# One program for the output projection, the queries, the search and the expert rows of a two-layer hybrid block

## The reference, cut to what matters

```
x = x + mod[2] * (y @ w_out[l])
h2 = modulate(x, norm2_g[l], mod[3], mod[4])       # rms_norm * g * (1 + scale) + shift
q = (h2 @ wq).reshape(tb, 8, 2, 64)                # 8 heads, two halves
s1, s2 = q[:, :, 0] @ subkeys[0].T, q[:, :, 1] @ subkeys[1].T
v1, i1 = top_k(s1, 16);  v2, i2 = top_k(s2, 16)
top, pos = top_k(v1[:, None] + v2[None, :], 16)    # 16 of 256 candidates
eid = i1 * 128 + i2 at pos                         # 8 * 16 = 128 experts for a token
gate = softmax(top)
act = gelu(h2 . u[eid])
x = x + mod[5] * sum(gate * act * v[eid])
```

## Time and profile before

| | us |
|---|---|
| median of 3 runs (lowest, highest) | 5564.36 (5556.88, 5573.46) |
| the profiled execution, its time | 5550.64 |
| the profiled execution, its span | 5548.8 |
| DVE, PE, POOL busy in that span | 2761.7, 2600.2, 2996.4 |
| mean granted TensorE clock | 0.698 |

### The profile page before, as it was taken

How to read it: one execution, slowest core, us unless ns; L and a number is a source line. 1 busy time by engine, 2 the same in 40 slices (tenths; PEclk the granted TensorE clock), 3 DMA queues, 4 the chain that set the end, 5 groups by cost and what they waited for, 6 DMA issues and landing times. The chain is left out here.

```text
span 5548.8 us, 34331 instructions
## 1 busy us (share of the span) xinstructions
PE 2600.2 (47%) x10865; PEld 1112.8 (20%) x10865; DVE 2761.7 (50%) x6111; ACT 493.1 (9%) x1044; POOL 2996.4 (54%) x2702
## 2 busy tenths in 40 slices
PE   6976787203333333333333569668600333333344
PEld 2435554100000000000000134355400000000001
DVE  1136644896556466465443011554598655644410
ACT  0025430000000000000000000443000000000000
POOL 1001201687777777777777620130178777777765
PEclk9987998656565565666666789789855655565567
DMA  5401011799999999999999941011189999999998
GB/s 187 144 23 18 2 40 50 278 336 378 387 377 378 377 370 375 377 378 385 376 380 365 365 169 61 8 19 40 43 311 329 366 361 371 363 371 367 369 367 322
DMA packets 450113, 1468.11 MB, mean 265 GB/s; under 512 B 59226, under 2 KB 97326, under 8 KB 446862
## 3 DMA queue, kind: packets, MB, share of 16 engines
q0 software_dynamic: 368640, 1342.34, 64.1%
q1 hardware_dynamic: 70280, 99.62, 5.6%
q10 hardware_dynamic: 11014, 23.95, 1.4%
HBM read 1459.62 MB, written 6.13 MB: 264 GB/s over the span
## 5 line engine op out<-in xcount | busy, mean ns | idle before, releaser
L1738 DVE CUSTOM_DVE_ANT_0 peer_U<-peer_U,peer_H 128x1024 f32<-128x1024 f32 x1280 | 1564.4, 1223 | 1326.5 <-DMA peer_U<-in_peer_u_dram,peer_expert 1235.4
L1704 PE MATMUL tile_acc<-peer_V,peer_spread 128*32 128x512 f32 x4544 | 977.2, 998 | 1821.4 <-DMA peer_V<-in_peer_v_dram,peer_turned 1730.7
L1603 POOL DMA_INDIRECT peer_U<-in_peer_u_dram,peer_expert x1280 | 1376.9, 1076 | 571.5 <-issue 389.3
L1618 POOL DMA_INDIRECT peer_V<-in_peer_v_dram,peer_turned x1136 | 1253.5, 1103 | 490.3 <-issue 329.2
L1704 PEld LDWEIGHTS tile_acc<-peer_V,peer_spread 128*32 128x32 f32 x4544 | 190.0, 153 | 2538.0 <-issue 2537.4
L371 PE MATMUL proj_acc<-proj_w,HT 128*128 128x512 f32 (+2 forms) x1280 | 485.7, 539 | 2.9 <-DVE PR L426 2.9
L741 POOL MEMSET glascore_Q<- 128x8192 f32 x2 | 13.8, 6925 | 559.5 <-POOLq L101 559.5
L371 PEld LDWEIGHTS proj_acc<-proj_w,HT 128*128 128x128 f32 x1280 | 241.6, 190 | 244.2 <-issue 213.1
L1281 POOL TENSOR_TENSOR X<-X,out_part 128x512 f32<-128x512 f32 x20 | 25.3, 1265 | 457.4 <-DVE out_part L1271 457.4
L426 DVE COPY PR<-proj_acc 128x512 f32<-128x512 f32 (+2 forms) x80 | 49.5, 622 | 404.6 <-PE proj_acc L371 404.6
L1430 PE MATMUL tile_keys<-peer_sub,peer_QT 64*128 64x128 f32 x256 | 37.6, 442 | 406.4 <-DVE peer_rest L1448 330.0
(11 more groups left out here) (261 smaller groups left out, 3305.5 us busy)
## 6 DMA issues: line engine op xcount, KB each, us to landing
peer_ada<-in_ada_w_dram SPq DMA_DIRECT2D x24, 1024.0 KB
proj_w<-in_w_in_dram SPq DMA_DIRECT2D x10, 2048.0 KB, 8.0
peer_U<-in_peer_u_dram,peer_expert POOLq DMA_INDIRECT x1280
peer_V<-in_peer_v_dram,peer_turned POOLq DMA_INDIRECT x1136
proj_ada<-in_ada_w_dram ACTq DMA_DIRECT2D x16, 1024.0 KB, 4.8
setup_ada<-in_ada_w_dram SPq DMA_DIRECT2D x8, 1024.0 KB, 17.3
out_w<-in_w_out_dram SPq DMA_DIRECT2D x2, 4096.0 KB, 14.8
query_w<-in_peer_wq_dram SPq DMA_DIRECT2D x4, 2048.0 KB, 15.9
```

What stands on the lines that cost most here:

```text
L1603: pool.indirect_dma_start(s.U[:, n % RING], None, u_rows, bass.IndirectOffsetOnAxis(ap=s.expert[:, j % 2, k:k + 1], axis=0)).then_inc(ug[n ...
L1618: pool.indirect_dma_start(place, None, v_rows, bass.IndirectOffsetOnAxis(ap=s.turned[:, i % 2, e:e + 1], axis=0)).then_inc(done, 16)
L1704: mm = nc.tensor.matmul(acc[32 * c:32 * c + 32, i % 2, half], s.spread[:, e * 32:e * 32 + 32], v_slot(V * GROUP + c)[0][:, 512 * half:512 ...
L1738: nc.vector.tensor_tensor_reduce(out=s.U[:, n % RING], in0=s.U[:, n % RING], in1=s.H[:, tiles[j]], scale=1.0, scalar=0.0, op0=ALU.mult, op ...
```

## The change

`out_project`, `peer`, `peer_queries` and `peer_tiles` become one stage `experts`; `norm_modulate` stays for the input projection only. `layer` calls it while Y is allocated:

```diff
-        out_project(nc, m, l, t0, Y)
-        if stop == "out":
-            return
-    peer(nc, m, l, t0)
+        experts(nc, m, l, t0, Y)
```

The rings lend their memory to the weights (`w_out` lies in U, `wq` in V), H is written over Y, and PSUM banks are shared. The loads stand in one SP stream; POOL waits for the last output product and the first tile's expert numbers:

```diff
+        w_out, wq = s.U, s.V
+        s.H = Y
+        out_acc, turn = acc[:, 0], acc[:, 1]
+        order = [("y", 0), ("y", 1), ("h", 0), ("y", 2), ("h", 1), ("y", 3), ("h", 2)]
+        for i in range(4, T):
+            order += [("y", i), ("h", i - 1)]
+        order += [("h", T - 1)]
+        place = {what: n for n, what in enumerate(order)}
...
             def _(pool):
+                pool.wait_ge(prods, 2 * T)
                 for n in range(FIRST_V + V_ALL):
                     j, k = n // SLOTS, n % SLOTS
-                    if n == 2 * RING:
-                        nc.gpsimd.memset(s.spread[:], 0.0).then_inc(zeroed, 1)
+                    if n == ZERO_AT:
+                        pool.wait_ge(qprods, 2 * T)
+                        nc.gpsimd.memset(s.spread, 0.0).then_inc(zeroed, 1)
                     if n < U_ALL:
-                        if j and k == 0:
-                            pool.wait_ge(sems.chosen, j)
+                        if k == 0:
+                            pool.wait_ge(sems.chosen, j + 1)
...
             def _(sp):
+                sp.dma_start(gain[:], row_bcast(m.a["diff_norm_g"][l])).then_inc(gains, 16)
+                for half, sem in ((0, w_in), (1, w_in2)):
+                    cols = slice(512 * half, 512 * half + 512)
+                    sp.dma_start(w_out[:, :, cols], m.a["w_out"][l].rearrange("(k p) n -> p k n", p=P)[:, :, cols]).then_inc(sem, 16)
+                for x in range(2):
+                    sp.dma_start(gate_row[:, x], row_bcast(mod_row(m, l, 1 - x, 2))).then_inc(gate_in, 16)
+                sp.dma_start(sub_rows, m.a["peer_subkeys"][l].rearrange("s n d -> n s d")).then_inc(key_in, 16)
+                sp.dma_start(g, row_bcast(m.a["norm2_g"][l])).then_inc(coef_in, 16)
+                for x, stream in enumerate(norm_streams):
+                    sp.dma_start(sc[:, x], row_bcast(mod_row(m, l, 1 - stream, 4))).then_inc(coef_in, 16)
+                for x, stream in enumerate(norm_streams):
+                    sp.dma_start(sh[:, x], row_bcast(mod_row(m, l, 1 - stream, 3))).then_inc(shift_in, 16)
+                for half, sem in ((0, wq_in), (1, wq_in2)):
+                    cols = slice(512 * half, 512 * half + 512)
+                    sp.dma_start(wq[:, :, cols], m.a["peer_wq"][l].rearrange("(k p) n -> p k n", p=P)[:, :, cols]).then_inc(sem, 16)
```

PE has a list written out by hand. `project_out(i, half)` is eight products of 512 columns, `transposes` eight transposes into one PSUM place shared by y and h, `scores(i, step)` is `key_scores`, `QUERIES_AT` is `[1, 5, 9, 13]`, and `queries(i)` makes all heads of one tile, so with 128 moving columns:

```diff
+                def transposes(kind, i):
+                    n = place[kind, i]
+                    if n:
+                        pe.wait_ge(ev0, n)
+                        pe.wait_ge(ev1, n)
+                    if kind == "h":
+                        pe.wait_ge(hs, i + 1)
...
+                def project_out(i, half):
+                    n = place["y", i]
+                    pe.wait_ge(ev0, n + 1)
+                    pe.wait_ge(ev1, n + 1)
+                    if i == 0:
+                        pe.wait_ge(w_in if half == 0 else w_in2, 16)
+                    else:
+                        pe.wait_ge(scaled1, 2 * i - 1 + half)
...
+                        for c in range(4):
+                            h = 4 * b + c
+                            for k in range(KD):
+                                mm = nc.tensor.matmul(bank[:, c * P:(c + 1) * P], wq[:, k, h * P:(h + 1) * P],
+                                                      HT[:, k, tiles[i] * P:(tiles[i] + 1) * P], start=k == 0, stop=k == KD - 1)
...
+                pe.wait_ge(key_in, 16)
+                nc.tensor.transpose(ps[:, 0, 0:NKEYS], s.cand[:, 0:NKEYS], m.ident).then_inc(ytrs, 1)
+                transposes("y", 0)
+                transposes("y", 1)
+                project_out(0, 0)
+                project_out(0, 1)
+                project_out(1, 0)
+                transposes("h", 0)
+                queries(0)
+                pe.wait_ge(subbed, 1)
+                scores(0, 0)
+                project_out(1, 1)
+                transposes("y", 2)
+                project_out(2, 0)
+                scores(0, 1)
+                project_out(2, 1)
+                transposes("h", 1)
+                transposes("y", 3)
+                scores(0, 2)
+                project_out(3, 0)
+                project_out(3, 1)
+                scores(0, 3)
+                transposes("h", 2)
+                for i in range(4, T):
+                    transposes("y", i)
+                    project_out(i, 0)
+                    project_out(i, 1)
+                    transposes("h", i - 1)
+                transposes("h", T - 1)
+                queries(1)
                 for G in range((FIRST_V + V_ALL) // GROUP):
...
+                    if j == 0 and g in QUERIES_AT and QUERIES_AT.index(g) + 2 < T:
+                        queries(QUERIES_AT.index(g) + 2)
```

DVE does residual and normalisation of each tile itself and puts pieces of `retrieve(0)` between them:

```diff
+                def residual(i):
+                    t = tiles[i]
+                    for half in range(2):
+                        dve.wait_ge(prods, 2 * i + half + 1)
+                        nc.vector.tensor_tensor(half_out[:, half], out_acc[:, half],
+                                                gate_row[:, 0 if t < CT else 1, half * 512:(half + 1) * 512], ALU.mult).then_inc(scaled1, 1)
+                        dve.wait_ge(scaled1, 2 * i + half + 1)
+                        x = m.X[:, t, half * 512:(half + 1) * 512]
+                        nc.vector.tensor_tensor(x, x, half_out[:, half], ALU.add).then_inc(added1, 1)
+                def normalise(i):
+                    dve.wait_ge(squared, i + 1)
+                    nc.vector.tensor_scalar(stat[:, 1, i:i + 1], stat[:, 0, i:i + 1], 1.0 / D, EPS, ALU.mult, ALU.add).then_inc(mean, 1)
+                    yield
+                    dve.wait_ge(root, i + 1)
+                    link(nc.vector.reciprocal(stat[:, 1, i:i + 1], stat[:, 2, i:i + 1]))
+                    link(nc.vector.scalar_tensor_tensor(out=Y[:, t], in0=m.X[:, t], scalar=stat[:, 1, i:i + 1], in1=sc[:, x],
+                                                        op0=ALU.mult, op1=ALU.mult))
+                    nc.vector.tensor_tensor(Y[:, t], Y[:, t], sh[:, x], ALU.add).then_inc(hs, 1)
+                def tile(i, n):
+                    pieces(n)
+                    residual(i)
+                    pieces(1 if n else 0)
+                    for _ in normalise(i):
+                        pieces(1 if n else 0)
...
+                tile(0, 0)
+                evacuate("h", 0)
+                for i in range(4, T):
+                    norm_heads(i)
+                tile(1, 8)
+                evacuate("y", 2)
+                pieces(6)
+                tile(2, 8)
+                evacuate("h", 1)
+                evacuate("y", 3)
+                pieces(6)
+                tile(3, 8)
+                evacuate("h", 2)
+                for i in range(4, T):
+                    evacuate("y", i)
+                    tile(i, 14)
+                    evacuate("h", i - 1)
+                evacuate("h", T - 1)
+                for _ in finding:
+                    pass
```

366 lines of the change are left out of this document (165 added, 201 removed).

## The result

The changed kernel took 5503.14 us (median of 4 runs, 5493.37 to 5506.0), the kernel before 5560.9 beside it (5556.88 to 5573.46): ratio 0.9889, 95% interval 0.9868 to 0.991. That is 57.8 us less, and faster by more than the 0.3% that can be told from no change. The forecast was 5493, its range 5460 to 5532. The profiled execution took 5503.28, with a span of 5501.5, against the 5548.8 of the profiled execution before: 47.3 less.

A forecast was written before the change was run, and what follows sets the result against it. Expert gathers were taken as the bound, so gain came from earlier first gathers: 46.9 + 26.9 - 2 - 1 = 70.8 us, giving 5480 against the profiled execution and 5493 for the median, range 5460 to 5532.

The forecast's parts named there:

- what bounds the kernel: Expert gathers set the time once they flow; only the first gather's start and the first stretch's speed can move.
- sub-keys at 18.5, scores at 65: From the output stage's start: sub-keys land near 18.5 us, PE waiting for them; first scores at 65, before 149.6.
- Term of the queries: On PE, one tile's queries are 128 instructions at 0.13 us each: 16.6 us, or 18.6 where PE was idle before.
- second and fourth rival: Queries beside dot products slow: 33 us a set, 5534, chance 0.14; or 64 us a set, 5745, chance 0.04.
- The page's figure: About 81 ns for a sustained 128-column matmul, giving 10.4 us for a tile's queries and a 5481 sum; not used.
- Term of the projection: On PE before the first gather: 6.9 us a half; layer 0's last products end at 165.1, first gather 181.6.
- The waits at each H: PE stands 5 to 8 us for each tile from the second on, because transposes share one place.
- Term of the first stretch: From layer 0's first gather: thin cover for the transposed expert numbers, about 89 against 90.4 us, charged 2 us.
- In layer 1 nothing: Layer 1's first stretch loses nothing: only two query sets remain, begun 33 us before the first gather.
- The sum: Layer 0 gain 46.9, layer 1 gain 26.9, less 2 for thin cover and 1 for semaphores: 70.8 us.
- First and third rival: DVE never kept waiting, gain 102, 5462, chance 0.10; PE and DVE taking turns throughout, no gain, 5564, chance 0.05.

The follow-up runs named there:

- b: Changed kernel with all queries made before the first gather instead of beside the dot products; 5349.1 us, ratio 1.0023 to the kernel before.
- c: Changed kernel with the first tile's queries, scores and search behind the last tile's projection; 5357.0 us, ratio 1.0044 to the kernel before.
- d: Changed kernel with the sub-keys loaded right behind the gain, ahead of w_out; 5241.9 us, ratio 0.9833 to the kernel before.
- e: Changed kernel with the evacuations of the next y and last H ahead of a tile's normalisation; 5235.7 us, ratio 0.983 to the kernel before.
- m: Changed kernel with sub-keys loaded first and evacuations ahead of the normalisation, without spread select passes; 5205.0 us, ratio 0.977 to the kernel before.
- n: Changed kernel with the next tile's search beginning at dot product 9, not 8, and select passes behind every second dot product; 5529.5 us, one run (before 5556.4).
- g: Changed kernel with the search for the next tile beginning at dot product 9 in place of 8; 5298.4 us, one run.
- p: Changed kernel with the select passes behind every second dot product instead of every one; 5272.0 us, ratio 0.9894 to the kernel before.
- k: Changed kernel with evacuations ahead of the normalisation and the next tile's search beginning at dot product 9, not 8; 5283.8 us, one run.

## Why the prediction was right, point by point

- **Right: what bounds the kernel.** The gathers kept their rate and the gain came at the first gathers, 40.6 and 25.5 us. b and c show that both parts of the change are needed: without the one or the other, the ratio is 1.002 or 1.004.
- **Right: sub-keys at 18.5, scores at 65.** They stood at 18.6 and 62.7. But I had put the new wait at "3 us past the old first product" (the sub-keys' landing), which leaves out what PE does between the sub-keys and its first product. Taking it away (d) gave 13.3 us a layer: the projection could have begun at 10, not 15.6. The wait was seen and priced too low.
- **Term of the queries.** 14.7 us before the search, where I took 16.6 (0.115 an instruction, not 0.13), and 14 to 17 beside the dot products; the cover held by 4 us at the expert numbers. The second and fourth rival (33 and 64 us a set) fall on this number. The granted clock of the first stretch is 0.70, where it was 0.55. The 1.00 of the earlier trace rows, which I took as evidence, was a stretch in which PE did not wait, so it said little of bursts behind a wait. Here two of four sets run at the upper level throughout, and two, soon behind waits of 10.4 and 7.1 us on the search, begin at the lower one, so that they are granted 0.86 and 0.90 over their whole length. The windows of `queries(2)` and `queries(4)`:

```profile
963.27:977.83 14.56, 14.56 (x130) 14.36 (x128) 12.42 (x29) 0.60 (x1) 11.82 (x10) 1.00 0.93 329
...
1022.90:1039.56 16.66, 16.66 (x130) 16.66 (x129) 16.66 (x51) 0.60 (x1) 13.61 (x11) 0.86 0.88 304
```

- **The page's figure.** The figure of the Trainium skill, "TensorE: Matmul & The Clock Gate", section "Back-to-back issue gap", would have made 10.4 of the 14.7.
- **Term of the projection, too low in layer 0.** The walk had 165.1 for tile 5's last product and it was 936.88 - 765.71 = 171.2, which is nearly the whole miss of the first gather (187.9 for 181.6). Tiles 4 and 5 took 15.38 and 16.31 us, where I had 13.8 each, because each begins at the lower level of the clock. Cut into two windows of equal length, tile 5 is granted 0.71 and then 1.00, and only 14 instructions stand in the first:

```profile
920.57:928.70 8.13, 8.13 (x14) 3.62 (x15) 7.78 (x23) 0.00 (x0) 0.00 (x0) 0.71 0.01 2
928.70:936.88 8.18, 8.18 (x22) 3.59 (x21) 5.38 (x6) 0.00 (x0) 0.00 (x0) 1.00 0.00 0
```

- The wait of 6.4 us is not needed for that. In e, tiles 3 and 5 have waits of 0.8 to 2.4 us before them and still took 15.90 and 16.73 us; e's tile 4 took 13.97. Shorter waits did not keep the clock up in every tile. From PE's timeline of e:

```profile
863.25 15.90 PE L1600 MATMUL experts_acc<-experts_U,experts_YT 128*128 128x512 f32 x32
...
902.53 16.73 PE L1600 MATMUL experts_acc<-experts_U,experts_YT 128*128 128x512 f32 x32 [0.83 <-ACT experts_YT L1519]
```

- The other 2 us of the miss are tile 4's later start: its transposes stood behind `scores(0, 3)`, for which PE waited 3.94 us on the search.
- **The waits at each H** ("5 to 8 us for each tile") were 6.4. I took them for part of the chain from product to H. They were an order of two lists: e removed most of each without removing any work, and the first gathers came 33.9 us earlier in sum.
- **Term of the first stretch, the mis-sized one.** I charged 2 us for thin cover on PE and the stretch grew by 10.6, for the most part, it seems, by long issues on POOL. The term's cause was wrong as well as its size. That it is not a cost of the queries is shown by m, which makes them at the same place with a stretch of 227.5. That the long issues make the difference rests on the five profiles with them (236.5 to 238.3) against the five without (227.5 to 231.0), on the 10.2 us estimated above, and on n, whose stretch is 6.9 below g's. Against it stands p, which took the long issues away and won 3.5.
- **"In layer 1 nothing"** was wrong by the one pair of profiles that there is: the first stretch there is 6.2 us longer. The kernel before has the shortest of all, 221.6, and was profiled once, so whether this is the change or chance stays open. b, with no queries beside the dot products, has 233.6, so the queries do not explain it.
- **The sum.** 46.9 + 26.9 - 2 - 1 = 70.8 was forecast. The same terms measured 40.6 + 25.5 - 10.6 = 55.5, against 57.8 between the medians. What is left between the two profiled executions is -10.9 in the other gathers (4.3 in layer 0, 6.6 in layer 1) and +2.7 elsewhere. The -10.9 stays unexplained: over the kernels above, layer 1's first stretch ranged from 221.6 to 234.2 us with no pattern that was found. That the medians are 57.8 apart, near the low end of the gain of 55 to 90, is in part luck: the two profiled executions are 47.3 apart, which is below it.
- **First and third rival.** DVE did stand for PE, so not 5462: from the first scores to the first gather it was 125.2 us, where DVE's own work is 99.5. Pieces did run beside products, so not 5564: the lockstep had the first gather at 235 us, and it came at 187.9.

## What to carry to other kernels

Making the first tile ready early pays only if the other tiles' preparation leaves the path as well: either half alone gave nothing here, both together 1.1%. When two engines answer each other in hand-written lists, look at what stands ahead of the evacuation that the other engine waits for, and at the first wait of the list; reordering those two was worth 69 us, where the change itself gave 60 in the same runs. Some 10 of the 69 are a stretch without long issues, which, by k, this order does not ensure; 59 are at the first gathers. Of work moved beside DMA-bound work, work out when it begins to delay something (doubling it is the test), and watch the issuing engine as well as the busy ones.

## What the runs showed of the hardware that was not expected

- An indirect DMA's issue on GpSimd, mostly 0.9 to 2.0 us and at most 4.1 elsewhere in these stretches, took 5.8 to 7.2 us in layer 0 (9.0 once in layer 1) while VectorE ran passes of 1.2 us with two SBUF inputs back to back, and ended 0.9 us into the next one-input reduction. The DMA share fell to 0.41 over 16 us in the changed kernel:

```profile
1092.32:1108.34 16.02, 0.00 (x0) 0.00 (x0) 15.26 (x22) 0.00 (x0) 15.41 (x3) 0.61 0.41 131
```

- Beginning the same work one dot product later brought this into a kernel that had not had it: the stretch went from 230.7 to 237.8 us.
- SyncE's queue stood 6.3 us at two gate rows of 512 KB right behind 4 MB of weights; a load of 64 KB queued behind them landed 18 us after the stage's start, and before 4 us when it went first.
- The same kernels, before and after alike, ran 4% faster in most of the experiments, for no cause that was found, with gathers at 402 in place of 377 GB/s; the ratios hardly changed (0.9889 and 0.9871).
